# A second pair of weight buffers in the third layer, and weight splits spread over the steps of a turn

## What is computed

```python
h = rms_norm(x, g_pre[l], NORM_EPS)
proj = jnp.einsum('bsd,dn->bsn', h, w_in[l])
qa, ka, va, fa, za, qb, kb, vb, zb, gates = jnp.split(proj, SPLIT_POINTS, axis=-1)
ya = fox_attention(split_heads(qa, FOX_HEADS), split_heads(ka, FOX_HEADS), split_heads(va, FOX_HEADS), log_f)
ya = merge_heads(ya) * jax.nn.silu(za)
yb = diff_attention(qd, kd, vd, lam)          # (softmax(q1 k1^T) - lam * softmax(q2 k2^T)) v, causal
yb = rms_norm(yb, g_subln[l], SUBLN_EPS) * (1.0 - lam_init)
yb = merge_heads(yb) * jax.nn.silu(zb)
gate_a, gate_b = jnp.split(jax.nn.sigmoid(gates), N_BRANCHES, axis=-1)
merged = (gate_a * jnp.einsum('bsw,wd->bsd', ya, w_branch[l, 0])
          + gate_b * jnp.einsum('bsw,wd->bsd', yb, w_branch[l, 1]))
y = jnp.einsum('bsd,de->bse', merged, w_out[l])
x = x + rms_norm(y, g_post[l], NORM_EPS)
```

## Time and profile before

| | us |
|---|---|
| median of three timed runs | 2463.62 |
| lowest and highest of them | 2461.63, 2466.01 |
| the profiled execution, its own time | 2458.4 |
| its span, from the first to the last instruction | 2456.6 |
| third layer: from about 1386 to the end | 1070 |
| of it the turns: from about 1480 to 2113 | 633 |

### The profile page before, as it was taken

One profiled execution on the slowest core, in us unless ns is written; L12 is line 12 of the kernel. 1 busy time (PEld: TensorE's weight loads), 2 busy tenths in 40 slices (PEclk: granted clock), 3 DMA queues, 4 the chain that ended last, 5 costly groups with the idle time before them and its releaser, 6 DMA issues. The chain is left out here.

```text
span 2456.6 us, 33964 instructions
## 1 busy us (share of the span) xinstructions
PE 2297.0 (94%) x11898; PEld 1836.7 (75%) x11898; DVE 1116.2 (45%) x3122; ACT 886.5 (36%) x2276; POOL 202.8 (8%) x315
## 2 busy tenths in 40 slices
PE   6999999999979997999989799999999999699998
PEld 5878788788767886777767687767777677688877
DVE  4345264253453115445543325566665665533342
ACT  4142241341332113455543224544444444423232
POOL 1000000000000000112210000010010100101013
PEclk9999999999999998999999899999999999899999
DMA  3111111111135113011134501111011102333322
GB/s 140 37 52 52 60 49 51 53 47 53 47 138 192 69 60 129 10 48 50 50 106 119 187 1 58 59 43 31 35 43 59 42 9 76 102 100 116 99 89 91
DMA packets 125298, 175.10 MB, mean 71 GB/s; under 512 B 7576, under 2 KB 73176, under 8 KB 123616
## 3 DMA queue, kind: packets, MB, share of 16 engines
q1 hardware_dynamic: 119088, 157.39, 19.4%
q10 hardware_dynamic: 6064, 15.84, 1.7%
HBM read 143.79 MB, written 29.42 MB: 71 GB/s over the span
## 5 line engine op out<-in xcount | busy, mean ns | idle before, releaser
L91 PE MATMUL heads_p_ps<-ret_w_second_hi_sb,ret_hT_hi_sb 128*128 128x512 f32 x384 | 150.6, 392 | 0.0
L91 PE MATMUL heads_p_ps<-ret_w_second_lo_sb,ret_hT_hi_sb 128*128 128x512 f32 x384 | 149.9, 390 | 0.0
L91 PE MATMUL heads_p_ps<-ret_w_second_hi_sb,ret_hT_lo_sb 128*128 128x512 f32 x384 | 149.6, 390 | 0.0
L91 PE MATMUL att_proj_ps<-br_w_second_hi_sb,br_hT_hi_sb 128*128 128x512 f32 x272 | 117.4, 432 | 2.6 <-DVE br_w_second_lo_sb L2168 2.6
L91 PE MATMUL att_proj_ps<-br_w_second_lo_sb,br_hT_hi_sb 128*128 128x512 f32 x272 | 106.8, 393 | 0.0
L91 PE MATMUL att_proj_ps<-br_w_second_hi_sb,br_hT_lo_sb 128*128 128x512 f32 x272 | 106.7, 392 | 0.0
L2128 ACT ACTIVATE br_x_sb<-br_x_sb,att_max_neg_sb 128x256 f32<-128x256 f32 (+7 forms) x128 | 97.8, 767 | 13.1 <-DVE att_max_neg_sb L2341 12.9
L2607 ACT ACTIVATE mrg_yT_hi_sb<-br_y_raw_sb 128x1024 fp32r<-128x1024 f32 x32 | 33.9, 1060 | 142.0 <-PE mrg_b_ps L2538 118.8
L91 PEld LDWEIGHTS heads_p_ps<-ret_w_second_lo_sb,ret_hT_hi_sb 128*128 128x128 f32 x384 | 72.2, 188 | 15.7
L91 PEld LDWEIGHTS heads_p_ps<-ret_w_second_hi_sb,ret_hT_hi_sb 128*128 128x128 f32 x384 | 72.5, 189 | 15.3
L91 PEld LDWEIGHTS heads_p_ps<-ret_w_second_hi_sb,ret_hT_lo_sb 128*128 128x128 f32 x384 | 72.3, 188 | 15.4
(11 more groups left out here) (471 smaller groups left out, 6508.9 us busy)
## 6 DMA issues: line engine op xcount, KB each, us to landing
early_w_kv_sb<-a_w_blocks SPq DMA_DIRECT2D x28, 1024.0 KB, 5.3
all_w_block_sb<-w_turns SPq DMA_DIRECT2D x12, 2048.0 KB, 9.2
br_y_raw_sb<-branch_yT_dram SPq DMA_DIRECT2D x32, 512.0 KB, 4.2
ret_o_dram<-early_x_rows_sb ACTq DMA_DIRECT2D x32, 256.0 KB, 2.4
all_w_block_sb<-swa_turns SPq DMA_DIRECT2D x4, 2048.0 KB, 9.5
ret_out_o_rows_sb<-ret_o_dram ACTq DMA_DIRECT2D x6, 1024.0 KB, 5.3
x_dram<-early_x_rows_sb SPq DMA_DIRECT2D x12, 512.0 KB, 2.9
heads_v_sb<-x SPq DMA_DIRECT2D x8, 512.0 KB, 4.4
```

The lines of the kernel that those rows point to most:

```text
L91: mm = pe.matmul(out, rows[a], w[b], start=(k == 0 and a + b == 0), stop=(k == KT - 1 and b == 1))
```

## The change

It does four things, all in the third layer.

1. `w_second` becomes two buffers, `w_second_fox` and `w_second_diff`, so that a whole block has two places.
2. The two batches of four splits a turn go. A table, `SPLIT_STEPS`, spreads the eight pieces of the next block but one over the steps of the present turn: two in step 1, two in step 2, one each in steps 3 to 6. On ACT they stand ahead of `exps`, on DVE at the end of the step. Only the first turn keeps its batch in step 0 as well.
3. The memory for this is taken from merge's buffers. `y_raw` is laid over `vz_fox`, `w_br_raw` over the last quarter of `x` (where the transposed probabilities stand), `w_br` over `w_second_fox`. So the first load of `w_br_raw` moves from step 2 to step 9 of the last diff turn, behind its last `values`.
4. In merge the splits in chunk 0 go (all eight pieces of chunk 1 were split in the last turn), and the load of chunk 2's gate weights (2 MB) moves from the start of chunk 1 to the very start of chunk 0, ahead of the row loads.

```diff
-        w_second = mem.parts("w_second", P, KT // 2, BANK)
+        w_second = {True: mem.parts("w_second_fox", P, KT // 2, BANK), False: mem.parts("w_second_diff", P, KT // 2, BANK)}
...
-        y_raw = mem.sb("y_raw", P, 2, 2 * PAIRS, P)
-        w_br_raw = mem.sb("w_br_raw", P, 2 * PAIRS, MERGE_COLS)
+        vz_fox = mem.sb("vz_fox", P, TILES, 2 * P)
+        y_raw = vz_fox[:].rearrange("p t n -> p (t n)").rearrange("p (b k n) -> p b k n", b=2, k=2 * PAIRS)
+        w_br_raw = x[:, 6:8, :].rearrange("p t n -> p (t n)").rearrange("p (k n) -> p k n", n=MERGE_COLS)
...
+SPLIT_STEPS = {1: (0, 1), 2: (2, 3), 3: (4,), 4: (5,), 5: (6,), 6: (7,)}
...
             def turn_sync(turn, prev, following):
                 for t in range(steps(following)):
                     before = ago(turn, prev, t, 2)
+                    if t == TILES + 1:
+                        sp.wait_ge(pv_done, turn.tiles(TILES))
+                        sp.dma_start(w_br_raw, merge_blocks(dram)[:, :, 0, :]).then_inc(ahead_in[2], 16)
...
-                    if not following and t == 2:
-                        sp.dma_start(w_br_raw[:], merge_blocks(dram)[:, :, 0, :]).then_inc(ahead_in[2], 16)
                     if not following and t in (4, 5):
 
+                        sp.wait_ge(pv_done, turn.tiles(0))
+                        sp.wait_ge(sz_done, turn.tiles(0))
...
-                at_least(act, proj_done, turn.tiles(-TILES if ks[0] == 0 else 0))
+                at_least(act, proj_done, turn.tiles(-TILES))
...
-                    if t == 0:
-                        split_high(following or GATES, range(4, KT))
+                    if t == 0 and turn.is_first():
+                        split_high(following, range(4, KT))
...
+                    if t in SPLIT_STEPS:
+                        split_high((following or GATES).next(), SPLIT_STEPS[t])
                     if t < TILES:
                         exps(t)
...
-                    if t == TILES - 2:
-                        split_high((following or GATES).next(), range(0, 4))
...
-                    if t == 0 and not turn.is_first():
-                        split_low(following or GATES, range(4, KT))
...
                         out_rows(*last)
-                    if t == TILES - 2:
-                        split_low((following or GATES).next(), range(0, 4))
+                    if t in SPLIT_STEPS:
+                        split_low((following or GATES).next(), SPLIT_STEPS[t])
...
-        w_br = mem.parts("w_br", P, 2 * PAIRS, QW)
+        w_br = [part[:].rearrange("p k n -> p (k n)").rearrange("p (k n) -> p k n", n=QW) for part in w_second[True]]
...
-                    if t == 0 and not c.is_at(0):
-                        sp.wait_ge(w_lo, c.times(KT, -KT // 2))
+                    if t == 0 and c.is_at(0):
+                        load_gates(c.plus(2))
+                    if t == 0 and not c.is_at(0) and not c.is_at(1):
+                        sp.wait_ge(w_lo, c.times(KT, -KT))
...
-                    if t in (0, 1) and c.is_at(0):
-                        split_gates(c.plus(1), range(KT // 2 + 2 * t, KT // 2 + 2 * t + 2))
```

More of the change, by code:

```diff
@@ L2438, in gate_w @@
         def gate_w(c, k):
-            return w_at(c.parity == 0, k)
+            return [part[:, k % (KT // 2), :] for part in (m_mem[c.parity == 0] if k < KT // 2 else w_second[False])]
         def merged_parts(t):
@@ L2456, in load_branches @@
             def load_branches(c):
[L2457 removed]
+                sp.dma_start(w_br_raw, w_branch[:, :, bass.ds(c.times(1), 1), :].rearrange("p k c n -> p k (c n)")).then_inc(wbr_in, 16)
             def load_rows(c, t):
```

21 lines of the change are left out of this document (9 added, 12 removed).

## The result

The changed kernel takes 2472.2 us in the median of twenty runs; the kernel before, measured again in the same rounds, takes 2461.8. The ratio is 1.0038, with a 95% interval of 1.0030 to 1.0046: slower by 0.4%, about 10 us.

A forecast was written before the change was run, and what follows sets the result against it. The prediction took a closed ring of DVE, ACT and POOL in diff turns to bound the kernel. Its terms, 4.2 + 2.6 + 3.0 + 2.3 + 0.3 + 0.5 = +12.9 us on 2463.6, gave 2476.5, range 2463 to 2484.

The forecast's parts named there:

- the ring: In a diff turn DVE, ACT and POOL wait for each other, none for PE; their summed work sets its length.
- the stall of 2.35: PE's 2.35 us wait in step 7 of a diff turn, behind ACT's four high splits; removing it brings nothing.
- Diff turns, +1.4 each: Loop's three diff turns: low splits ahead of `logits` add 2.3 us, less PE's lost wait of 0.88; +4.2 us in all.
- The high splits cost nothing in diff turns: Diff turns: high splits ahead of `exps` fit inside ACT's 0.60 us wait for DVE's row maximum; cost 0.
- The clock, +2.6: Start of the loop's three fox turns: half-clock stretches, 1.7 us lost each, taken at 0.5 of the chance; +2.6 us.
- Fox turns, +0.76 each: Four fox turns: high splits delay ACT's copy in steps 5 and 6, +1.1, less PE's 0.34 wait; +3.0 us in all.
- The last diff turn, +2.3: Last diff turn: its end follows the ring and nothing behind takes up the delay; 2.55 - 0.26 = +2.3 us.
- Merge, +0.8: Merge's start and chunk 0: loads issued in a new order delay a store and row loads; +0.3 and +0.5 us.
- The first part: Merge: 1 MB of branch weights issued ahead of the last store of y, which queues behind part of it; +0.3 us.
- The second: Merge, chunk 0: 2 MB of gate weights ahead of the row loads; third row load some 2 us later; +0.5 us.
- The rival of 3.5 us: Merge: the 2 MB ahead of the rows costs 3.5 us instead of 0.5, PE's clock falls again; 2481 us, chance 0.12.
- The load that comes too late: Step 1: block's pieces not there when ACT wants them, 1 us or more, seven times; 2483 us, chance 0.08.

The follow-up runs named there:

- the diff half: Undone in a run: the change, but the loop's three diff turns go back to batches of four splits; 2467.1 us, ratio 1.0025 to the kernel before.
- the kernel with the late gate weights: The change, but merge loads chunk 2's 2 MB of gate weights at the start of chunk 1 again; 2471.2 us.
- the kernel with the three moves: The change, with diff turns' low splits in DVE's waits, their high splits ahead of `copy_out`, and fox turns' high splits behind ACT's copies; 2448.2 us.

## Why the prediction held, and where it was off

The prediction was slower, 2476.5 (2463 to 2484), +12.9 us; measured are 2472.2 and +10.4. The signs that it named are there: steps 1 and 2 of a diff turn are longer by 1.2 and 1.0 us and steps 3 to 6 by 0.6 each, with no idle time between a split and `logits`. That the total comes out close is in part luck, since terms that were too large and too small offset each other (below). The range of 2466 to 2484 doesn't follow from the bounds of the terms either: added up they go from about -16 to +24 us, 2447 to 2488.

**What bounds the kernel** was right: the ring, and not the stall of 2.35. Undoing the diff half brings the stall back and makes the kernel faster; making the splits twice costs their full length.

**Diff turns, +1.4 each.** At PE's first matmul of the fox turn (1634.25 in the profile of the change, 1630.11 before) the delay grew by 2.1, 2.2 and 2.2 us a turn where 2.3 was forecast, and the 0.88 behind it has gone: +1.2 to +1.4. Where the slow stretch stays away, the whole turn is +1.0 and +1.1 (first and third turn of the kernel with the late gate weights). The term is right to 0.4, which over three turns is +3.2 instead of +4.2.

**The high splits cost nothing in diff turns: right for the change, for a reason that was only half right.** I put them inside ACT's wait of 0.60. That wait was read in step 6 alone. In step 4 of the same turn of the kernel before, ACT's timeline has none:

```profile
1589.99 0.37 ACT L2116 ACTIVATE att_yT_sb<-att_o_ps,att_g_sub_scaled_sb 128x128 f32<-128x128 f32 x1 [2.56 <-PE att_o_ps L1987]
1590.31 0.83 ACT L2128 ACTIVATE br_x_sb<-br_x_sb,att_max_neg_sb 128x640 f32<-128x640 f32 x1
```

There the exponentials follow `copy_out` at once, and in steps 2 and 3 too. The high splits are covered in the change only because DVE's split makes the row maximum later by as much; where the low splits leave the ring, the high ones cost 1.9 us a turn.

**The clock, +2.6: right in the price of a stretch, wrong in the count.** From PE's first matmul in a fox turn of the loop to its first in step 1 it takes 9.5 us in the kernels without the batch where the clock stays at 1.00 and about 11.1 with a slow stretch of 3.4 us in it, with the same stall of 1.29 us ahead in both: 1.6, where 1.7 was forecast. In the first of these turns the profile of the change has a stretch twice as long, 6.83 us; the first diff turn of the table is +3.7 with it and +1.0 in the kernel with the late gate weights, so this one cost 2.7. The stretches, as length, busy time by engine, granted clock and DMA; first two of the change, then the kernel with the late gate weights at the place of the first:

```profile
1633.40:1640.23 6.83, 5.98 (x16) 4.74 (x17) 2.16 (x12) 1.49 (x6) 1.39 (x2) 0.50 0.00 0
1797.24:1800.65 3.41, 3.41 (x10) 2.67 (x9) 1.39 (x10) 0.00 (x0) 0.00 (x0) 0.50 0.00 0
```

```profile
1630.00:1637.00 7.00, 5.71 (x29) 4.59 (x28) 3.56 (x17) 3.03 (x14) 1.39 (x2) 1.00 0.04 11
```

What failed is the ledger: I counted stretches that would come and none that would go. The kernel before had one behind the loop's way back (1867.98), on PE's own path; the change has none there and got back 1.1 us in that place. Why it has none isn't shown; its turns are shifted in time, but so are those of kernels that have it. In the five kernels with each low split made once and ahead of `logits`, a slow stretch stood at the start of 11 of 15 fox turns, more than the half that I took. In the profile of the change the stretches that came cost 2.7 + 1.6 + 1.6 us, 1.1 went, and the output has 1.4 more: +6.2 in all. Less these, and less the 0.9 of the unchanged layers, the 17.7 us between the profiles are 10.6, and the medians are 10.4 apart. So this term was +6.2 in the one profile and about nothing in the medians, an estimate as good as the interval of the medians, which is 2 us to either side. I can't say which stretches a given run has.

The trace bears out again what the Trainium skill, "TensorE: Matmul & The Clock Gate", says in its part on the clock gate, that the gate isn't tied to the program: the same wait of 1.29 us at the same instruction was followed by a clock of 0.50 in one kernel and 1.00 in another.

**Fox turns, +0.76 each.** Measured +0.8 in each of the three, and all of it gone with the splits behind the copies. The make-up is near to the forecast: 0.44 more in step 5 and 0.51 more in step 6 (0.68 instead of 0.17), where two times 0.55 were counted; in step 7 a wait of 0.26 has come in place of the 0.34. The first fox turn cost 1.2, of which 0.5 lies ahead of its step 2, where POOL waited for a load of the decay row. That load runs beside the 2 MB block in both kernels; in the ten other profiles this place comes 0.3 to 0.9 us later than in that of the kernel before, and no run shows why.

**The last diff turn, +2.3.** Measured +2.1.

**Merge, +0.8.** The first part was forecast at +0.3 and measured at nothing: the small store behind the 1 MB of branch weights landed in 1.6 us, as always. Its line in the profile of the change, 2120 to 2150 us (count, size, median us from issue to landing), stands under those of the loads:

```profile
br_x_sb<-w_branch SPq DMA_DIRECT2D x2, 1024.0 KB, 7.7
all_w_block_sb<-w_turns SPq DMA_DIRECT2D x1, 2048.0 KB, 9.4
br_vz_fox_sb<-branch_yT_dram SPq DMA_DIRECT2D x4, 512.0 KB, 6.2
branch_yT_dram<-att_yT_sb SPq DMA_DIRECT2D x1, 64.0 KB, 1.6
```

The second, forecast at +0.5 for the 2 MB ahead of the rows, is the 1.2 us that PE stands idle more in chunk 0: the row load came 4.6 us later than its like in the kernel before (4.3 us from issue to landing there), not some 2. The rival of 3.5 us for it didn't come. The 0.7 us of PE's waits at the starts of chunks 2 and 3 were in no term.

The rule of the Trainium skill, "DMA: Bandwidth & Descriptors", in its section on queues, rings and completion order, that descriptors are consumed in ring order, agrees with the row load of 8.86 us, issued 2.4 us behind the 2 MB. With the store it made no difference here: it was issued 4.3 us behind a load that took 5.3, when only 1.0 us of it was left.

**The load that comes too late** (a rival at 0.08) didn't come: in the first fox turn ACT's first high split had no wait for SP's load, which was issued at 1480.18 and landed 10.1 us later, with 0.4 us to spare before the split at 1490.69.

**The total.** Without the clock the forecast was +10.3. By the stages it is 1.2 for the first fox turn, 3.2 for the diff turns, 2.4 for the other fox turns, 2.1 for the last turn, 1.3 for chunk 0 and 0.7 behind it, less 0.3 at the first way back: 10.6. The diff turns came out 1.0 smaller than forecast, merge 1.2 and the fox turns 0.6 larger.

## What to carry to other kernels

A stall of one engine is worth something only if the engines behind it aren't bound by something else; ask what it meets when it gets there earlier, and follow the engines whose rows have no idle time between two of them. Where work is spread to remove a batch, its place within the step decides: here, ahead of the instruction that closes a ring each piece costs its full length (0.60 of 0.62 us in step 6), and a few instructions further, in a wait for another engine, the same piece costs nothing (10.55 us a step against 10.53 without it). Two engines' additions at the same point of a ring can hide each other, as the 0.3, 1.6 and 3.5 us here do, so move both before judging either. And before a stage's time is laid to an edit, its granted clock is to be read beside it: the late load in chunk 0 took away 1.9 us of idle PE, but the chunk was only 0.9 us shorter, at a clock of 0.92 instead of 0.96.

## What the runs showed of the hardware that I had not expected

A stall of 1.29 us at the same matmul is followed by PE at half clock in one kernel and at full clock in another whose program up to there is the same; it is worth 1.6 us each time for a stretch of 3.4 us, and in one profile it was a stretch of 6.8 us and 2.7. The stretch up to the third layer's first turn, whose program is the same in all kernels here, is 1472.1 to 1480.7 us long in eleven profiles, which is more than many edits are worth. The 64 KB store that was issued 4.3 us behind a 1 MB load wasn't held up (1.6 us), while a 512 KB load 2.4 us behind a 2 MB load took 8.86 instead of 3.9. DVE's low splits of 0.68 us in its wait for ACT's exponentials cost ACT nothing that the step's length shows. Whether they would slow POOL's power (0.70 us) no run shows, since the splits placed ahead of it had ended before it began (1580.36 + 0.68 and 1581.29 in the kernel with the three moves).
